# Expert rounds of a two-block transformer kernel: gather from split tokens, one scatter operand, and a new bank plan

## What is computed

```python
def hierarchical_moe(u, w_router_group, w_router_expert, w_gate, w_up, w_down):
    x = u.reshape(B_ * S_, D)                      # 256 x 1024
    ...                                            # each token: one group of 8 experts, its best 2
    combine = (g_onehot[:, :, None] * (p_g[:, :, None] * w_in_group[:, None, :])).astype(x.dtype)
    y = jnp.zeros_like(x)
    for g in range(N_GROUPS):
        hid = jax.nn.silu(jnp.einsum('nd,edf->nef', x, w_gate[g])) * jnp.einsum('nd,edf->nef', x, w_up[g])
        y = y + jnp.einsum('nef,efd->nd', hid * combine[:, g, :, None], w_down[g])
    return y.reshape(B_, S_, D)
```

## Time and profile before

| | |
|---|---|
| median of 3 runs | 2799.12 us (2795.89 to 2800.32) |
| the profiled execution | 2798.28 us, of which the span (first to last instruction) 2796.5 us |
| mean granted clock of TensorE | 0.933 of 2.4 GHz |
| busy, share of the span | PE 89%, DVE 71%, ACT 46%, POOL 1% |
| expert rounds, first layer | from 242 us to 855 us |
| expert rounds, second layer | from 1078 us to 1691 us |
| one round in the middle of them | 38.0 us |

### The profile page before, as it was taken

The page is one execution under the profiler, slowest core; times in us unless marked ns, Lnnn a source line. Parts: engine busy times, 40 slices in busy tenths (PEclk is TensorE's granted clock), DMA queues, the critical chain, the costliest instruction groups (busy, mean ns, idle before and its releaser), DMA issues.

```text
span 2796.5 us, 30491 instructions
## 1 busy us (share of the span) xinstructions
PE 2476.5 (89%) x11306; PEld 1800.7 (64%) x11306; DVE 1998.8 (71%) x2495; ACT 1287.6 (46%) x1409; POOL 23.9 (1%) x45
## 2 busy tenths in 40 slices
PE   7987999999998977999999996889799667977898
PEld 6556777777774545777777773656499424833787
DVE  3737898988893547889988885165887544368875
ACT  3235777777772325777777760144233111100432
POOL 0000000000000000000000000000000000000000
PEclk9997999999998987999999998899899768988899
DMA  8323877778856313877777857220755701305460
GB/s 306 121 98 151 337 322 323 322 324 353 345 225 249 120 60 151 353 323 322 323 323 336 360 210 290 92 91 31 286 211 211 242 8 56 135 28 198 171 262 25
DMA packets 116505, 607.80 MB, mean 217 GB/s; under 512 B 5300, under 2 KB 8428, under 8 KB 91644
## 3 DMA queue, kind: packets, MB, share of 16 engines
q1 hardware_dynamic: 111536, 588.83, 53.4%
q0 software_dynamic: 4880, 17.76, 1.8%
HBM read 605.51 MB, written 1.05 MB: 217 GB/s over the span
## 4 chain that ended last, share of the span: by engine, by line
PE 69%; DVE 21%; issue 4%; ACT 4%; DMA 1%; DVEq 0%; POOL 0%; ACTq 0%; SPq 0%
PE bank L860 9%; PE bank L1084 9%; PE bank L1132 8%; DVE slab_parts L2320 7%; PE bank L1108 7%; PE bank L872 4%; PE bank L1073 4%; PE bank L959 2%; PE bank L1328 2%; PE bank L1330 2%; PE bank L1329 2%; PE bank L1341 2%; PE bank L1343 2%; PE bank L1098 2%; PE bank L1342 2%
## 5 line engine op out<-in xcount | busy, mean ns | idle before, releaser
L2320 DVE TENSOR_TENSOR slab_parts<-ring,high 128x2048 fp32r<-128x2048 f32 x384 | 858.9, 2288 | 54.7 <-ACT high L1635 52.7
L1635 ACT ACTIVATE high<-ring 128x2048 fp32r<-128x2048 f32 x384 | 729.3, 1910 | 226.5 <-DMA ring<-in_moe_w_gate 120.9
L1084 PE MATMUL bank<-high,xT_parts 128*128 128x512 f32 x1024 | 287.4, 403 | 10.2 <-DVE xT_parts L2347 9.4
L1084 PE MATMUL bank<-slab_parts,xT_parts 128*128 128x512 f32 x1024 | 278.3, 394 | 0.0
L1479 ACT ACTIVATE arena<-bank 128x512 f32<-128x512 f32 (+4 forms) x162 | 89.4, 586 | 361.0 <-PE bank L860 99.5
L860 PE MATMUL bank<-ring,xT 128*128 128x512 f32 (+3 forms) x576 | 238.4, 575 | 11.0 <-DVE xT L1954 7.1
L1627 ACT ACTIVATE arena<-bank 128x512 f32<-128x512 f32 (+1 forms) x352 | 190.6, 552 | 103.0 <-PE bank L1108 66.7
L1132 PE MATMUL bank<-arena 128*128 128x512 f32 x512 | 225.2, 592 | 1.5 <-ACT arena L1627 1.5
L1084 PEld LDWEIGHTS bank<-high,xT_parts 128*128 128x128 f32 x1024 | 189.2, 190 | 52.5 <-DVE xT_parts L2347 9.7
L1084 PEld LDWEIGHTS bank<-slab_parts,xT_parts 128*128 128x128 f32 x1024 | 193.6, 189 | 44.6
L860 PEld LDWEIGHTS bank<-ring,xT 128*128 128x128 f32 x576 | 111.3, 194 | 134.9 <-issue 123.3
(11 more groups left out here) (357 smaller groups left out, 3538.8 us busy)
## 6 DMA issues: line engine op xcount, KB each, us to landing
ring<-in_moe_w_gate SPq DMA_DIRECT2D x64, 2048.0 KB, 11.8
ring<-in_moe_w_up SPq DMA_DIRECT2D x64, 2048.0 KB, 16.2
ring<-in_moe_w_down SPq DMA_DIRECT2D x64, 2048.0 KB, 8.6
ring<-in_mlp_w SPq DMA_DIRECT2D x32, 2048.0 KB, 13.0
ring<-in_w_mod SPq DMA_DIRECT2D x24, 2048.0 KB, 8.0
ring<-in_even_w_in SPq DMA_DIRECT2D x7, 2048.0 KB, 21.5
ring<-in_odd_w_in SPq DMA_DIRECT2D x6, 2048.0 KB, 23.0
ring<-in_h_w_in SPq DMA_DIRECT2D x6, 2048.0 KB, 8.1
```

What stands on the lines that cost most here:

```text
L1084: last = mm(dst[:, :], seated2[:, 4 * half + k, e], part_[:, k, :], start=(half == a == k == 0), stop=(half == a == 1 and k == 3))
L1635: act_fn(hi, weight_half(layer, name, half), ACT.Copy).then_inc(sem(f"high{layer}"), 1)
L2320: v.tensor_tensor(low, w, hi.bitcast(F32), ALU.subtract)\
```

## The change

It works on the rounds in six ways, and both layers run it.

1. **Gather.** The normed tokens are split once for each layer: ACT writes `u_high`, DVE `u_low` (two instructions of 128 x 1024 each). The gather multiplies both with `sel` in fp32r, 32 matmuls of 128 columns into 4 fillings instead of 16 fp32 ones into 2. What lies in PSUM is then already the high and the low part, and ACT copies it as it is, in 4 copies; DVE's two subtractions are gone. The gather is cut in pieces that stand around the two halves of down0.
2. **Down rows.** Both parts of a down filling (64 partitions each) were scattered. Now ACT copies the low rows (64 partitions, `low_rows`), and DVE adds the high rows from PSUM to them into `pair_y` (`add_rows`, 4 in a round); expert 0 fills partitions 0 to 63 of `pair_y`, expert 1 the others.
3. **Scatter.** So one operand holds the rows of both experts: 2 transposes instead of 4, 4 fp32 matmuls instead of 8. They add up in banks 4 to 7 over all 16 rounds, and DVE adds the banks to h once, after the last.
4. **Banks.** All other fillings share banks 0 to 3 by a new table.
5. **Waits.** The experts count on semaphores of their own.
6. **Loads.** SP loads the first 6 slabs of the following stage from inside the experts, each as soon as PE is through with the slab it replaces.

```diff
-FILLS = (("gate0", 0), ("up0", 1), ("down1.0", 2), ("down1.1", 3), ("fold0", 4), ("turn", 5), ("gate1", 6), ("up1", 7),
-         ("out0", 0), ("out1", 1), ("out2", 2), ("out3", 3), ("down0.0", 4), ("down0.1", 5), ("gather0", 6),
-         ("gather1", 7), ("fold1", 2))
+FILLS = (("gate0", 1), ("up0", 2), ("down1.0", 0), ("down1.1", 3), ("fold0", 1), ("turn", 2), ("gate1", 0), ("up1", 3),
+         ("gather0", 2), ("gather1", 0), ("down0.0", 1), ("gather2", 3), ("down0.1", 2), ("gather3", 0), ("fold1", 3))
+OUT_BANKS = (4, 5, 6, 7)
...
+                    refill_short(PAIRS - 1)
+                    for name in ("gate0", "up0", "gate1", "up1", "down0", "down1"):
+                        used_short(name, PAIRS)
+                        next_stage(SLAB_OF[name])
...
-                                last = mm(dst[:, c * P:(c + 1) * P], u_by_eight[:, t, k, :], sel[:, t, :],
+                                last = mm(dst5[:, c, :, a], u_parts[a][:, t, 2 * j + c, :], sel[:, t],
                                           start=(t == 0), stop=(t == 1))
...
-                    for j in range(4):
-                        u, dst = enter(f"out{j}", r)
-                        for e in range(2):
-                            c = (e * NT + j // 2) * P
-                            last = mm(dst[:, :], weightedT[:, c:c + P], pair_y[e][:, (j % 2) * 512:(j % 2 + 1) * 512],
-                                      start=(e == 0), stop=(e == 1))
-                        tell(last, u)
+                    for j, bank in enumerate(OUT_BANKS):
+                        ins = mm(banks[bank][:, :], weightedT[:, (j // 2) * P:(j // 2 + 1) * P],
+                                 pair_y[:, (j % 2) * 512:(j % 2 + 1) * 512], start=first, stop=last)
...
-                    down(0, r)
                     if not last:
-                        gather(r)
+                        gather(0, r)
+                        gather(1, r)
+                    down(0, r, 0)
+                    if not last:
+                        gather(2, r)
+                    down(0, r, 1)
+                    if not last:
+                        gather(3, r)
...
+                for t in range(NT):
+                    act.wait_ge(sem("tile_normed"), 2 * (2 * layer + 1) + t + 1)
+                    act_fn(u_high[:, t * D:(t + 1) * D], u_buf[:, t * D:(t + 1) * D], ACT.Copy)\
+                        .then_inc(sem("u_high"), 1)
...
+                def add_rows(e, half, r):
+
+                    u, ps = filled(f"down{e}.{half}", r)
+                    hs = slice(half * 512, (half + 1) * 512)
+                    dve.wait_ge(sem(f"low_rows{layer}"), r * 4 + (half + 1 - 2 * e))
+                    v.tensor_tensor(pair_y[e * SEATS:(e + 1) * SEATS, hs], low_rows[SEATS:P, hs], ps[0:SEATS, :],
+                                    ALU.add).then_inc(moe_drained[layer][u.bank], 1)
...
-                    if not first:
-                        scatter(r)
-                    if not last:
-                        seated_low(r)
+                    add_rows(0, 0, r)
+                    add_rows(0, 1, r)
+                    refill("down0", r, first, last)
+                    if not last:
+                        filled("gather3", r)
                         take_seats(r + 2)
-                    refill("down0", r, first, last)
```

406 lines of the change are left out of this document (224 added, 182 removed).

## The result

| | kernel before | changed kernel |
|---|---|---|
| time, median (lowest to highest), us | 2797.51 (2794.47 to 2800.32), 4 runs | 2765.09 (2762.77 to 2766.83), 4 runs |
| ratio, 95% interval | 1 | 0.9884 [0.9867, 0.9901] |
| profiled execution, its span, us | 2798.28, 2796.5 | 2765.13, 2763.1 |
| fold0 of round 1 to fold0 of round 15, us | 531.85 | 525.31 |
| so a round, us | 37.99 | 37.52 |

The forecast was 2688 us, with a range of 2650 to 2742. The change is faster by 1.2%, 32 us, where 110 were forecast: the direction was right, the size was not, and the range did not hold the time. A round, forecast at 35.0, takes 37.5.

What follows compares the result with a forecast made beforehand. PE bounded the kernel, with DVE and ACT close behind. Rounds falling from 37.99 to 35.0 us, plus head and tail, gave 99 us over two layers, the exit 11: 2798.3 less 110 is 2688 us, range 2650 to 2742.

Steps and rivals of the forecast that it cites:

- The prices of PE's work: PE in a round: scatter halved, 3.43 us saved; two transposes fewer, 0.1; gather 3.6; PE's sum 36.78 to 33.2.
- The dear gather: Rival, chance 0.12: the fp32r gather costs as much as 512 columns, 7.5 us a round; time 2755 us.
- the slower rival: Rival, chance 0.04: weight load and matmul no longer overlap in the gather, 15 us a round; time 2957 us.
- The split of the tokens: Head of each layer: two ACT copies and two DVE subtractions, made while PE is on the router; cost nothing.
- The loop: Round bound through gate0's load, ACT and PE: 35.0 us instead of 37.99, 1.8 over PE's sum.
- Gate0, up0 and down1 then take 7.47 + 3.73 = 11.2: Last part of the loop: PE from gate0's start at 23.85 us to the next mark at 35.05.
- A copy takes 0.48 by pace and 0.58 by itself; I take 0.53: ACT's part of the loop: four high halves of 1.81 us and seven copies, together 10.95 us.
- The mark to the load: First part of the loop: from the start of fold0 until the next gate0 is loaded, 12.8 us.
- ACT's wait for gate0's load shrunk from 4.27 to 2 to 3 us: Sign expected in each round of the later profile if the forecast held.
- the rival by 358 GB/s: Late loads: two slabs take 11.7 us, round 37.0, time 2744 us; given 0.03 of the 0.12 late case.
- The exit: Behind the second experts: slabs loaded in advance, next stage starts at 1692.7, ends at 1725.2 us; 10.8 us saved.
- Head and tail: Each layer outside its 14 rounds: 6.7 us from the tail, about 1 from the first gather.

Runs made afterwards that it cites:

- twice the gather: Changed kernel with each gather made twice, the second pass overwriting the first with the same values; 2774.96 us.
- the two small edits: Changed kernel with low-rows copies over 128 partitions and three filler matmuls in PE's wait ahead of gate0; 2707.24 us.
- fill: Changed kernel with six extra fp32r matmuls of 512 columns on PE in the wait ahead of gate0; 2715.22 us.
- rows128: Changed kernel with ACT's copies of down's low rows made over all 128 partitions instead of 64; 2713.04 us.
- leave: Changed kernel without PE's last wait, for the four last additions, before it leaves the experts' branch; 2757.57 us.
- gorder: Changed kernel with the last gather and its copy moved ahead of down0.1; 2742.57 us.
- three: Changed kernel with gate0 and up0 loaded ahead of down1, last gather ahead of down0.1, and low-rows copies over 128 partitions; 2714.21 us.

## Why the prediction was wrong

- **Direction, and the bound before: right.** PE bounded the kernel before; turning its loads changed nothing.
- **The prices of PE's work: right.** Scatter and the first half of the gather take 522.90 to 528.07, 5.17; less 16 x 0.111 the scatter has 3.4. The gather's 32 instructions take 3.6, 0.111 each (twice the gather started its rows of 4 every 0.445). The dear gather and the slower rival fell at once. The split of the tokens stayed hidden beside the router.
- **The loop: right in its shape.** fold0, load of gate0, ACT's eleven operations, gate0 to down1. With the two small edits the rounds at full clock took 35.06, as forecast.
- **"Gate0, up0 and down1 then take 7.47 + 3.73 = 11.2": the step that failed.** It took its prices at full clock, and the same text had PE wait one to two us ahead of gate0 in every round. In the changed kernel that wait brings half clock, and 1.65 us more. The stretch took 12.82, which is 1.6 a round and 45 us of the 78 that were missing; at full clock it took 11.2, as forecast ("fill", "rows128"). "fill" gave 1.67 x 28 = 47 us back. No row of the kernel before showed this wait; its waits of 1.2 us were split over down1, and the clock stayed at 1.00. I had no term for the clock in the rounds, and no rival either. The Trainium skill, "TensorE: Matmul & The Clock Gate" (HAM oscillation), describes such a loop, a wait in each turn after which the next turn starts at half clock, but with longer waits and little work between them. Here the turn did start at half clock, after a wait of 1.36 us in a round of 37.5; the measurement decides.
- **"A copy takes 0.48 by pace and 0.58 by itself; I take 0.53": mis-sized.** 0.53 was under the 0.62 of copies beside those of 64 partitions, and the high halves there take 1.94, not 1.81: the chain took 11.75 instead of 11.05, 0.7 in all, 20 us.
- **The mark to the load: 12.95 instead of 12.8**, 4 us in 28 rounds. The sign "ACT's wait for gate0's load shrunk from 4.27 to 2 to 3 us" did not come: it was 3.8 on the mean. The queue ran at 436 GB/s in these rounds, so the rival by 358 GB/s fell too. The Trainium skill has both figures: "Perfetto Trace Analysis" (Engine Utilization, a note) calls 358 GB/s a core's share with its pair's other core active, and gives a core alone about 435, which the trace agrees with. My rival took the first for a kernel that runs on one core.
- **The exit: 6.3 instead of 10.8.** The step "it starts when DVE has spread its vector" left out PE's own start, 3.4 us later; in the earlier trace rows 7.14 us of issue stood there, and I read them as time that the slab's load took. The slab was indeed late there (DVE waited for it until 1697.19), so that the start-up underneath could not be seen. The other 1.1 are 0.7 more up to PE's operand and 0.4 more for the first slab. "leave" gave 3.5 us back.
- **Head and tail: 6.7 and 6.9 us instead of 7.7.** From the row that gives the count of tokens to the last addition, layer 0 took 13.3 less and layer 1 13.8, of which 6.5 and 6.9 are the 14 rounds.

Together, in the profiled executions: 13.3 + 13.8 in the layers, 6.3 behind the second experts, 3.3 between the layers, where nothing was forecast; less 3.8 that the first layer started late. That start is chance: over the profiles of all these kernels ScalarE's first high half lies anywhere between 229.9 and 236.1, the latest in the kernel before with turned loads. The 3.3 may be chance too: in the profiles of the other versions this stretch takes anything from 206.1 to 212.4 us, 211.8 in the kernel before and 208.5 in the changed one. The sum is 33, as measured. Of the 78 us that were missing to 110, the half clock has 45, ACT's chain 20, the load 4 and the exit 4.5; the rest is head and tail, rounding and the late start, less what the stretch between the layers gave.

## What to carry to other kernels

When a change takes work from the engine that bounds, what comes next is a wait, and a wait on TensorE can have a second price, the clock: look where the freed time will stand in one piece, and cost what follows it at 1.2 GHz as one case. A loop across engines is to be summed with the pace of each very shape, in order of the program, and at its end a version with the loop's smallest terms mended is worth a run: 0.8 us less on ScalarE brought 2 us a round. And "issue" ahead of the first instruction behind a branch can hide a cost that stays when the wait beside it goes.

## What the hardware showed that I had not expected

- TensorE's clock fell to half for 3.4 us in each of 28 rounds, within 0.7 us of the end of a wait of 1.36 us, with TensorE busy 94% of the rounds, and in none of them with three or six extra matmuls in that wait. Nearly the same wait (1.27 us) with more work behind it brought it in 18 of 28 rounds. Neither the waits nor the busy share decide alone: "gorder" and "three" both have waits of 1.1 and about 0.9 us in each round and are busy 94% of it, and half clock came in 15 of 28 rounds of the one and in one of 28 of the other. What decides in a given round stays open.
- On ScalarE each step beside a copy of 64 partitions is 0.13 to 0.15 us longer than between operations of 128: copying twice the rows took 0.8 us from a chain with two such copies (11.77 to 10.95).
- An fp32r matmul of 128 columns with a new 128 x 128 weight takes 0.111 us, much the same as one instruction of an fp32 matmul with 128 x 128 weights and 64 (0.111) or 128 columns (0.112), and little under the 0.12 of 256 columns in fp32r.
- TensorE needed 6.0 us from its last wait in a branch to the first matmul behind it, and started with its operand, 3.4 us after its last matmul in the branch, when that wait was left out.
